# Hybrid attention laid out by row tile instead of by pair of heads, with the first tile's projection and expert choice between the second tile's jobs

## The chip, the cores and the metric

One core of a Trainium2 chip. The metric is the device time of the whole kernel in microseconds (us); lower is better.

## What is computed

A three-layer block on x of 256 tokens by 1024 features, all in float32. Layers 1 and 2 (differential attention, block attention, each with a squared-ReLU MLP) are untouched. Layer 3 is the hybrid layer:

```python
proj = rmsnorm(x, norm1_gain) @ w_in
o_a  = nsa_mixer(...)      # 8 heads: compressed, selected and window branches, gated
o_b  = mla_mixer(...)      # 8 heads over low-rank q and kv
mixed = concat([rmsnorm(o_a), rmsnorm(o_b)]) @ w_out
h = x + mixed
return h + peer_ffn(rmsnorm(h, norm2_gain), w_q, sub_keys, u, v)
```

`peer_ffn` does this for each of 256 tokens and 8 heads: a query (256 wide, RMS-normed), scores against two sets of 128 keys, the best 16 of each, the best 16 of the 256 sums, hence 16 experts out of 16384; then `sum_k softmax_k * gelu(x . u[e_k]) * v[e_k]`.

## The kernel before

Tokens are handled in two row tiles of 128. The engines have programs written out by hand, bound together by named semaphores; the order in each program is the order of work on that engine.

**Hybrid attention.** The eight selected and window head pairs and the four low-rank head pairs are 12 units (`nsa_unit`, `mla_unit`). A unit holds two heads m and three 128x128 blocks for each: tile 0 against keys 0, tile 1 against keys 0 and 1. TensorE's loop over u = 2..13 (L1137 on) turns the probabilities of unit u-2 (`turn_probs`, L632), makes the scores of unit u (`scores`, L623 and L625), and weighs the values of unit u-2 (`weigh`, L641 to L643), with one group of low-rank transposes (`turn_low_rank`, L1134) in eight of the steps. VectorE adds the mask and takes the row peak (`add_bias`, L1887), copies the turned probabilities of head 0 (L1901), inverts the totals (L2275, L2279) and scales the results into `nat` (`finish`, L2291, L2294). ScalarE takes the exponentials (L1279) and copies those of head 1 (L1285).

**Output projection and first choice** (`out_and_first_choice`, L916, and the start of `peer`, L958). The halves of the mixed rows are normed (ScalarE squares L1424, GpSimd power L1655, VectorE `out_scale` L2302), turned (L898) and multiplied by w_out: for each tile 16 matmuls of 128x512 (`out_product`, L906). Then for tile 0: add to `h` (L1993), turn (L863), query (L874), key scores (L889), and VectorE's choice (`first_choice`, L2458 to L2498), which names experts 0 to 7 (`first_names`, L2446) and then 8 to 15. Tile 1 goes through the same after its projection; its choice is laid between the dot products of tile 0's first unit (`unit`, L2520: key scores L2348, names L2423).

**The expert phase** (`peer`). There are 16 units (8 heads by 2 tiles), each of 16 gathers. One gather is an indirect DMA issued by GpSimd (L1772) of 128 rows of 8 KB, an expert's u and v side by side: 1.05 MB. There are 16 slots, one for each k. VectorE dots u with the row (L2506), ScalarE applies gelu (L1471) and makes a diagonal of the weights (L1459), TensorE adds v through it (`add_experts`, L838) and so frees slot k; the next unit's gather k waits for that (`v_used`) and for the names of its experts (`experts_ready`). SyncE also loads the 1.05 MB query weights of each further head (seven loads into ring slot 2, L379), the first when w_out is used up. The first unit's gathers are issued in `first_unit` on GpSimd (L1787), in an order that follows which slots are free:

```python
po.wait_ge(sem("experts_ready"), ...)    # experts 0..7 of tile 0
gather(0, 0..3); power(...); row_rms(1); gather(0, 4..7)
po.wait_ge(sem("experts_ready"), ...); po.wait_ge(sem("w_out_used"), ...)
gather(0, 8..10); po.wait_ge(sem("peer_q_done"), 4); gather(0, 11); power(...)
gather(0, 12..15)
```

## Time and profile before

| | us |
|---|---|
| Median of 3 runs | 1463.73 (1460.67 to 1466.08) |
| The profiled execution, its own time | 1461.87 |
| Its span, first to last instruction | 1460.1 |
| TensorE busy | 1323.1 (91%) |
| VectorE busy | 944.3 (65%) |
| ScalarE busy | 549.5 (38%) |
| GpSimd busy | 358.4 (25%) |

The profiled execution's time is its span plus 1.8 us around it. Busy shares are means over stages that differ: the MLPs and projections to about 700 us, the hybrid attention from 708 to 760 us, projection and first choice to about 828 us, the expert phase to the end.

### The profile page before, as it was taken

What the parts mean: (1) busy time and instruction counts of PE and PEld (TensorE: products, weight loads), DVE (VectorE), ACT (ScalarE), POOL (GpSimd) and SP (SyncE); (2) the same over time, 40 slices, a digit from 0 to 9 for tenths busy, and PEclk for the clock granted to TensorE, in tenths of its full rate; (3) what the DMA queues carried; (4) which work ended last, traced back from release to release, by engine and by line L of the source; (5) the groups of instructions that cost most, each with busy time, mean ns of one, the idle gap of its engine ahead of it and who ended that gap; (6) DMA issues with size and microseconds to landing.
All of it is one profiled execution on the core that took longest, in us unless ns stands there. A gap on an engine that the chain in (4) does not pass through costs nothing.

```text
span 1460.1 us, 19575 instructions
## 1 busy us (share of the span) xinstructions
PE 1323.1 (91%) x6461; PEld 934.2 (64%) x6461; DVE 944.3 (65%) x2283; ACT 549.5 (38%) x1131; POOL 358.4 (25%) x372
## 2 busy tenths in 40 slices
PE   8999999999999999999999789797887979788877
PEld 6988999988988999977875435343343535343333
DVE  4687554564557555585764777776767777776755
ACT  4563544444555444454662122222222212222221
POOL 0104000000000000012402454435434344345440
PEclk9999999999999999999999899899999999999999
DMA  9614665545315565463403999999999999999997
GB/s 360 261 58 113 226 196 172 195 151 231 116 55 174 176 191 183 167 235 123 174 1 124 420 420 421 420 421 422 422 421 422 422 422 422 421 422 422 421 421 306
DMA packets 97534, 406.84 MB, mean 279 GB/s; under 512 B 6955, under 2 KB 44524, under 8 KB 60748
## 3 DMA queue, kind: packets, MB, share of 16 engines
q0 software_dynamic: 39552, 276.60, 46.1%
q1 hardware_dynamic: 57932, 129.60, 25.9%
q8 instruction: 28, 0.46, 0.1%
q14 instruction: 22, 0.18, 0.0%
HBM read 404.84 MB, written 1.07 MB: 278 GB/s over the span
## 4 chain that ended last, share of the span: by engine, by line
PE 51%; DMA 22%; issue 13%; DVE 9%; POOL 2%; ACT 2%; DVEq 0%; POOLq 0%; SPq 0%; ACTq 0%
DMA arena_u<-in_peer_uv,prob 20%; PE ps L685 12%; PE ps L686 12%; PE ps L687 12%; PE ps L838 6%; DMA uv_gain<-in_peer_uv,prob 2%; PE ps L906 1%; DVE arena_u L2506 1%; PE ps L632 1%; PE ps L812 1%; PE ps L625 1%; PE ps L641 1%; DVE prob L2382 1%; DVE prob L2370 1%; PE ps L623 1%
## 5 line engine op out<-in xcount | busy, mean ns | idle before, releaser
L1860 DVE TENSOR_TENSOR w_low<-ring,w_high 128x1024 fp32r<-128x1024 f32 x140 | 165.2, 1221 | 151.3 <-ACT w_high L1222 150.8
L1222 ACT ACTIVATE w_high<-ring 128x1024 fp32r<-128x1024 f32 x140 | 140.7, 1052 | 171.8 <-PE ps L687 171.8
L838 PE MATMUL ps<-arena_u,sco 128*128 128x512 f32 x256 | 126.8, 648 | 36.1 <-ACT sco L1459 36.1
L685 PE MATMUL ps<-hT_high,w_high 128*128 128x256 f32 x512 | 145.0, 283 | 0.9 <-DVE hT_low L1853 0.9
L686 PE MATMUL ps<-hT_low,w_high 128*128 128x256 f32 x512 | 144.9, 283 | 0.0
L687 PE MATMUL ps<-hT_high,w_low 128*128 128x256 f32 x512 | 144.8, 283 | 0.0
L1471 ACT ACTIVATE prob<-prob 128x4 f32<-128x4 f32 (+2 forms) x67 | 13.8, 206 | 343.5 <-DVE prob L2506 343.5
L1459 ACT ACTIVATE sco<-const,prob 128x128 f32<-128x128 f32 x256 | 84.7, 392 | 155.1 <-DVE prob L2516 137.4
L1661 POOL TENSOR_SCALAR small<-small 128x1 f32<-128x1 f32 x8 | 4.3, 533 | 499.2 <-ACT arena_v L1254 499.2
L838 PEld LDWEIGHTS ps<-arena_u,sco 128*128 128x128 f32 x256 | 52.3, 208 | 102.7 <-issue 57.0
L838 PE MATMUL ps<-arena_v,sco 128*128 128x512 f32 x256 | 117.7, 592 | 0.0
L2506 DVE CUSTOM_DVE_ANT_0 arena_v<-arena_v,nat 128x1024 f32<-128x1024 f32 x64 | 78.4, 1226 | 57.4 <-DMA arena_v<-in_peer_uv,prob 56.8
L1772 POOL DMA_INDIRECT arena_u<-in_peer_uv,prob x64 | 75.8, 1185 | 157.7 <-DVEq L2425 67.2
L838 PE MATMUL ps<-ring,sco 128*128 128x512 f32 x192 | 89.9, 619 | 20.4 <-ACT sco L1459 20.4
L838 PE MATMUL ps<-uv_gain,sco 128*128 128x512 f32 x128 | 76.3, 752 | 34.4 <-ACT sco L1459 34.4
L2506 DVE CUSTOM_DVE_ANT_0 arena_u<-arena_u,nat 128x1024 f32<-128x1024 f32 x64 | 78.5, 1226 | 37.6 <-DMA arena_u<-in_peer_uv,prob 36.5
L685 PEld LDWEIGHTS ps<-hT_high,w_high 128*128 128x128 f32 x512 | 98.1, 192 | 2.4 <-DVE hT_low L1853 1.3
L686 PEld LDWEIGHTS ps<-hT_low,w_high 128*128 128x128 f32 x512 | 98.2, 192 | 1.0
L687 PEld LDWEIGHTS ps<-hT_high,w_low 128*128 128x128 f32 x512 | 98.2, 192 | 0.0
L685 PE MATMUL ps<-w_high,act_high 128*128 128x512 f32 x240 | 94.7, 394 | 0.0
L686 PE MATMUL ps<-w_low,act_high 128*128 128x512 f32 x240 | 94.3, 393 | 0.0
L687 PE MATMUL ps<-w_high,act_low 128*128 128x512 f32 x240 | 93.7, 391 | 0.0
(440 smaller groups left out, 2955.7 us busy)
## 6 DMA issues: line engine op xcount, KB each, us to landing
ring<-in_w_up SPq DMA_DIRECT2D x32, 1024.0 KB, 5.5
ring<-in_w_down SPq DMA_DIRECT2D x32, 1024.0 KB, 4.8
qkring<-in_qk_a SPq DMA_DIRECT2D x8, 1024.0 KB, 7.1
qkring<-in_qk_b SPq DMA_DIRECT2D x8, 1024.0 KB, 4.9
ring<-in_peer_wq SPq DMA_DIRECT2D x7, 1024.0 KB
ring<-in_w_in SPq DMA_DIRECT2D x8, 860.0 KB, 5.5
ring<-in_w_out_a SPq DMA_DIRECT2D x4, 1024.0 KB, 15.6
ring<-in_v_b SPq DMA_DIRECT2D x4, 1024.0 KB, 6.9
```

Source lines behind the costliest of these rows:

```text
L623: pe.matmul(ps[banks[m]][:, 0:P], q(m)[:, 0:P], k(m)[:, 0:P], start=True, stop=True)
L625: pe.matmul(ps[banks[m]][:, P:384], q(m)[:, P:S], k(m)[:, 0:S], start=True, stop=True)\
L632: last = pe.transpose(ps[2 + m][:, k * P:(k + 1) * P], prob[:, b, m, k * P:(k + 1) * P], ident)
L685: pe.matmul(dst, a[0], b[0], start=start, stop=False, skip_group_check=True)
L686: pe.matmul(dst, a[0], b[1], start=False, stop=False, skip_group_check=True)
L687: return pe.matmul(dst, a[1], b[0], start=False, stop=stop, skip_group_check=True)
L838: last = pe.matmul(ps[2 * t + n][:, :], diag[:, k % N_DIAG, :], slots[k][:, D + n * HALF:D + (n + 1) * HALF], start=False, stop=(final and ...
L1222: sc.activation(w_split[pair][0][:, part], ring[:, slot, part], ACT.Copy)\
L1459: sc.activation(diag[:, k % N_DIAG, :], ident, ACT.Copy, scale=weight[:, 16 * t + k:16 * t + k + 1])\
L1772: po.indirect_dma_start(slots[k], None, T["peer_uv"], bass.IndirectOffsetOnAxis(ap=expert[:, 16 * t + k:16 * t + k + 1], axis=0))\
L1860: ve.tensor_tensor(w_split[pair][1][:, part], ring[:, slot, part], w_split[pair][0][:, part].bitcast(F32), ALU.subtract)\
L2506: ve.tensor_tensor_reduce(row, row, nat[:, t, :], 1.0, 0.0, ALU.mult, ALU.add, dots[:, k:k + 1])\
```

## The change

The attention is cut into 18 jobs (`job_parts`). Jobs 0 to 5 hold tile 0 alone, two units in each (four blocks of 128x128); jobs 6 to 17 hold tile 1, one unit in each (two heads by 256 keys). All turned probabilities of a job go through one PSUM bank and one ScalarE copy of 512 columns; VectorE copies none. Scores of every job use the same two PSUM banks, so TensorE waits for the masking of the job before. Tile 0's norms, projection, row norm, query, key scores, choice and first gathers are laid into the steps of tile 1's jobs; tile 0 is turned and scored 128 columns at a time. Tile 1's last half, its rows, query and choice follow in `last_rows` and `first_unit`. The slots are renumbered so that the first gathers go where the attention holds nothing. The choice's scratch, the key scores' banks and ScalarE's outputs of the squares move to other buffers. The expert phase from the second unit on is the same. The core of the diff (ScalarE's loop over the jobs, which mirrors TensorE's, and the small helpers are left out):

```diff
-        slots = [au[:, 2048 * r:2048 * r + 2048] for r in range(4)]
-        slots += [uv_proj[:, :], av[:, 4096:6144], uv_mk[:, 0, :], uv_mk[:, 1, :], ring[:, 0, :], ring[:, 1, :], ring[:, 3, :],
-                  first_wq, uv_gain[:, 0, :], uv_gain[:, 1, :], av[:, 6144:8192], av[:, 0:2048]]
+        slots = [au[:, 0:2048], au[:, 6144:8192], av[:, 4096:6144], av[:, 6144:8192], au[:, 2048:4096], au[:, 4096:6144],
+                 uv_proj[:, :], uv_mk[:, 0, :], uv_mk[:, 1, :], uv_gain[:, 0, :], av[:, 0:2048], ring[:, 0, :], ring[:, 1, :],
+                 ring[:, 3, :], first_wq, uv_gain[:, 1, :]]
...
+        def job_parts(j):
+            if j < FIRST_JOBS:
+                return [(x, 2 * j + x // 2, x % 2, x * P, (x + 1) * P) for x in (0, 2, 1, 3)]
+            return [(m, j - FIRST_JOBS, m, m * S, (m + 1) * S) for m in range(2)]
...
+            def last_rows():
+                pe.wait_ge(sem("finished"), count.take("finished"))
+                for n, bank in enumerate((2, 3)):
+                    turn_keys(range(2 + 4 * n, 6 + 4 * n), bank)
+                turn_out(1, 1, 6)
+                turn_keys(range(10, 14), 1)
+                turn_keys(range(14, 2 * P_HEADS), 0)
                 pe.wait_ge(sem("out_turned"), count.take("out_turned"))
+                for n in range(2):
+                    out_products(1, n, 4 + n, 1)
                 pe.wait_ge(sem("acc_ready"), count.take("acc_ready", 4))
                 pe.sem_inc(sem("w_out_used"), 1)
                 pe.sem_inc(sem(f"ring{PEER_SLOT}_used"), 1)
+                turn_rows(1, (7, 6))
+                first_queries(1, (4, 5), lambda c: hT[:, c, P:S])
+                pe.wait_ge(sem("pq_ready"), count.take("pq_ready", 4))
+                first_squares(1, 7)
+                first_scores(1, 6)
...
+                def job_scores(j):
+                    t = 0 if j < FIRST_JOBS else 1
+                    if j:
+                        pe.wait_ge(sem("sco_ready"), count.take("sco_ready", len(job_parts(j - 1))))
+                    parts = sorted(job_parts(j))
+                    for x, u, m, a, z in parts:
+                        q, k, _ = units[u]
+                        last = pe.matmul(score_places(j)[x], q(m)[:, t * P:(t + 1) * P], k(m)[:, 0:z - a], start=True, stop=True)
+                        if x >= len(parts) - 2:
+                            last.then_inc(sem("scores_ready"), 1)
...
+                def weigh_job(j):
+                    pe.wait_ge(sem("probT_a"), count.take("probT_a"))
+                    if j >= 2:
+                        pe.wait_ge(sem("finished"), count.take("finished"))
...
+                for step in range(2, N_JOBS + 2):
+                    j = step - 2
+                    if step == 9:
+                        turn_out(1, 0, 3)
+                    turn_job(j)
+                    if step in (4, 5):
+                        wait_low_rank(2)
+                    if step == MLA_JOB:
+                        wait_low_rank()
+                    if step == MLA_JOB + 2:
+                        wait_low_rank()
+                    if step < N_JOBS:
+                        job_scores(step)
+                    if step == 8:
+                        pe.wait_ge(sem("keysT_ready"), count.take("keysT_ready"))
+                        turn_out(0, 0, 3)
+                    if step == 12:
+                        pe.wait_ge(sem("pq_ready"), count.take("pq_ready", 4))
+                        first_scores(0, 0)
+                    if step == 18:
                         pe.wait_ge(sem("out_turned"), count.take("out_turned"))
+                        out_products(1, 0, 4, 0)
+                    if step == 19:
+                        out_products(1, 1, 5, 0)
+                    weigh_job(j)
+                    if step == 3:
+                        pe.wait_ge(sem("mqk_ready"), count.take("mqk_ready", 2))
+                        turn_low_rank(0, 0, 0)
+                        turn_low_rank(1, 0, 1)
+                    if step == 4:
+                        turn_low_rank(2, 0, 3)
+                        turn_low_rank(3, 0, 0)
+                    if step == 5:
+                        turn_keys((0, 1), 3)
+                    if step == 8:
+                        for n in range(2):
+                        pe.wait_ge(sem("out_turned"), count.take("out_turned"))
+                        for n in range(2):
+                            out_products(0, n, n, 0)
+                    if step == 9:
+                        pe.wait_ge(sem("out_turned"), count.take("out_turned"))
+                        for n in range(2):
+                            out_products(0, n, n, 1)
+                    if step == 10:
+                        turn_rows(0, (3, 0))
+                    if step == 11:
+                        first_queries(0, (1, 3), lambda c: hT_first[:, c, :])
+                    if step == 12:
+                        first_squares(0, 3)
+                        turn_low_rank(0, 1, 1)
+                    if step == 13:
+                        wait_low_rank()
+                        turn_low_rank(1, 1, 1)
+                    if step == 14:
+                        turn_low_rank(2, 1, 1)
+                    if step == 15:
+                        wait_low_rank()
+                        turn_low_rank(3, 1, 1)
+                    if step == 17:
+                        pe.wait_ge(sem("key_scores_taken"), count.take("key_scores_taken"))
+                        turn_out(0, 1, 3)
+                last_rows()
...
+            def last_rows():
+                half_squares(1, 1)
...
+                gates_of(0, scale=ms_out[:, 0:1])
+                row_squares(1)
+                take_rows(1, 6)
+                first_queries(1, (4, 5))
+                gelu_of(0, 4)
+                diagonals(0, range(4), first=True)
...
+                po.wait_ge(sem("c_out"), count.take("c_out", 2))
                 po.wait_ge(sem("experts_ready"), count.take("experts_ready"))
                 alone()
                 for k in range(4):
                     gather(0, k)
                 power(ms_out[:, 0:1], ms_in[:, 0:1], "ms_ready", "rms_ready")
+                po.wait_ge(sem("m_turned_a"), count.take("m_turned_a", 8))
+                for k in range(4, 6):
+                    gather(0, k)
+                half_rms(1)
+                count.skip("weighed", 2 * N_LAYER_UNITS)
+                po.wait_ge(sem("weighed"), count.take("weighed", N_JOBS))
+                gather(0, 6)
+                half_rms(3)
+                gather(0, 7)
+                po.wait_ge(sem("experts_ready"), count.take("experts_ready"))
+                gather(0, 8)
+                po.wait_ge(sem("keysT_ready"), count.take("keysT_ready", 6))
+                alone()
+                for k in range(9, 11):
+                    gather(0, k)
+                po.wait_ge(sem("w_out_used"), count.take("w_out_used"))
+                for k in range(11, 14):
+                    gather(0, k)
                 row_rms(1)
                 po.wait_ge(sem("peer_q_done"), count.take("peer_q_done", 4))
                 alone()
+                gather(0, 14)
                 power(ms_out[:, 1:2], ms_in[:, 1:2], "ms_ready", "rms_ready")
                 po.wait_ge(sem("rows_scaled"), count.take("rows_scaled"))
+                gather(0, 15)
...
+                for step in range(2, N_JOBS + 2):
+                    j = step - 2
+                    if step == 10:
+                        add_out(0, 0)
+                    job_share(j)
+                    if step < N_JOBS:
+                        job_bias(step)
+                    if step == 7:
+                        out_scale(0, 0)
+                    if step == 8:
+                        out_scale(1, 0)
+                    if step == 12:
+                        first_choice_begun()
+                    if step == 17:
+                        out_scale(0, 1)
+                    finish_job(j)
+                    if step in (5, 7, 15):
+                        ve.sem_inc(sem("norm_due"), 1)
+                    if step == 10:
+                        take_rows(0, 3)
+                    if step == 13:
+                        then(row_scale(0))
+                        first_query_rms(0)
+                        first_choice_ended()
+                    if step == 15:
+                        ve.wait_ge(sem("rms_ready"), count.take("rms_ready"))
+                        ve.tensor_scalar(neg_top, top[:, 0:1], ms_out[:, 0:1], -1.0, ALU.mult, ALU.mult)\
+                            .then_inc(sem("top_ready"), 1)
+                ve.sem_inc(sem("norm_due"), 1)
+                dot(0, 0)
+                dot(0, 1)
+                out_scale(1, 1)
+                dot(0, 2)
+                dot(0, 3)
+                dot(0, 4)
+                add_out(1, 4)
+                take_rows(1, 7)
+                gates_in(0)
+                dot(0, 5)
+                row_scale(1).then_inc(sem("rows_scaled"), 1)
+                dot(0, 6)
+                weights_of(0, 0, 4)
+                first_query_rms(1)
...
+            def first_unit():
+                dot(0, 7)
+                first_key_scores(1)
+                first_eights(1)
+                second_eights()
+                best_pairs()
+                dot(0, 8)
+                weights_of(0, 4, 8)
+                next_pairs()
+                pick(0)
+                pick(1)
+                name_experts(1)
+                for k in range(9, 13):
+                    dot(0, k)
```

## Rows read from the trace of the kernel before

**Rows 1.** The page, 40 equal slices: what the DMA engines moved.

```profile
GB/s 360 261 58 113 226 196 172 195 151 231 116 55 174 176 191 183 167 235 123 174 1 124 420 420 421 420 421 422 422 421 422 422 422 422 421 422 422 421 421 306
```

**Rows 2.** Stretches: PE, PEld, DVE, ACT, POOL busy, PEclk, DMA share, GB/s.

```profile
720.00:740.00 20.00, 19.98 (x174) 17.30 (x173) 16.97 (x89) 15.52 (x59) 0.00 (x0) 1.00 0.01 2
900.00:1000.00 100.00, 85.74 (x225) 41.62 (x224) 66.09 (x184) 22.80 (x66) 45.91 (x41) 0.93 1.01 421
```

**Rows 3.** Stretches of 2 us, gathers' begin and end, same columns.

```profile
790.00:792.00 2.00, 2.00 (x8) 1.04 (x8) 1.64 (x14) 0.00 (x0) 1.70 (x2) 1.00 0.46 66
792.00:794.00 2.00, 1.84 (x5) 0.53 (x3) 1.78 (x11) 0.00 (x0) 1.39 (x3) 1.00 0.76 279
...
1448.00:1450.00 2.00, 0.73 (x3) 0.27 (x2) 0.99 (x4) 0.90 (x3) 0.00 (x0) 1.00 0.38 156
```

**Rows 4.** Timeline of POOL: first gather of the first two units.

```profile
789.75 1.10 POOL L1772 DMA_INDIRECT arena_u<-in_peer_uv,prob  x1 [9.00 <-DVEq L2448]
...
828.02 1.26 POOL L1772 DMA_INDIRECT arena_u<-in_peer_uv,prob  x1 [11.19 <-DVEq L2425]
```

**Rows 5.** The chain of waits: start, us, what it ran on.

```profile
723.62 0.66 PE ps L632 x6
724.27 0.42 PE ps L623 x4
724.69 0.43 PE ps L625 x4
...
725.49 0.22 PE ps L642 x2
...
726.61 0.44 PE ps L1134 x4
...
742.12 0.87 PE ps L625 x4
...
767.67 6.87 PE ps L906 x16
...
779.07 3.57 PE ps L874 x32
```

**Rows 6.** Timeline of DVE: tile 0's choice, first and second part.

```profile
784.95 0.49 DVE L2458 MAX8 prob<-ps 128x8 f32<-128x128 f32 x2
...
788.61 0.17 DVE L2446 SCALAR_TENSOR_TENSOR prob<-prob 128x8 uint32<-128x8 f32 x1
788.96 0.06 DVE L2326 MEMSET small<- 128x1 f32 x1 [0.18 <-DVE prob L2446]
...
795.19 0.17 DVE L2446 SCALAR_TENSOR_TENSOR prob<-prob 128x8 uint32<-128x8 f32 x1
```

**Rows 7.** Groups by line, 700 to 835 us: busy us, mean ns.

```profile
L1417 ACT ACTIVATE hT<-ps 128x512 f32<-128x512 f32 x4 | 2.4, 591 | 5.1 <-PE ps L898 5.1
...
L2506 DVE CUSTOM_DVE_ANT_0 arena_u<-arena_u,nat 128x1024 f32<-128x1024 f32 x4 | 4.9, 1226 | 0.1
```

**Rows 8.** Timeline of PE and DVE, attention's start to tile 1's names.

```profile
716.73 0.87 PE L632 MATMUL ps<-const,prob 128*128 128x128 f32 x6 [0.79 <-DVE nat L2266]
...
760.10 1.10 DVE L2294 TENSOR_SCALAR nat<-ps,share 128x64 f32<-128x64 f32 x4 [2.66 <-PE ps L643]
...
763.14 0.66 PE L898 MATMUL ps<-const,nat 128*128 128x128 f32 x4 [1.38 <-DVE nat L2302]
...
790.16 3.68 PE L906 MATMUL ps<-ring,hT 128*128 128x512 f32 x8
...
811.20 0.48 DVE L2348 TENSOR_SCALAR sco<-ps,small 128x256 f32<-128x256 f32 x1 [3.96 <-POOL small L1655]
...
826.89 0.17 DVE L2423 SCALAR_TENSOR_TENSOR prob<-prob 128x16 uint32<-128x16 f32 x1
```

**Rows 9.** Stretches of 1 us: PE busy us, PEclk, DMA share, GB/s.

```profile
815.00:816.00 1.00, 0.00 (x0) 0.50 1.02 426
...
824.00:825.00 1.00, 1.00 (x2) 0.57 1.01 418
```

391 lines of the change are left out of this document (178 added, 213 removed).

## The prediction

> **What bounds the kernel now.** I read the page first. Its row of DMA rates stands at 420 to 422 GB/s in every slice from the 23rd to the 39th and was far lower before [rows 1]: from about 800 us to the end the gathers fill the DMA engines, while in the same stretch TensorE is busy 85.7 of 100 us and VectorE 66 [rows 2]. So the expert phase is a stream with a fixed amount left to carry, and the end moves only with the time at which the stream runs and with the gaps in it. One gather, or one load of query weights, is 1.05 MB, at 421.5 GB/s 2.49 us. There are 256 gathers and 7 loads: 263 pieces, 654 us. In the stretches of 2 us where it starts the engines move 66 and 279 GB/s, in the two together 2.4 us less than at full rate, so the full rate counts from 792.4 us; in 1448 to 1450 they move 156 GB/s, so it ends near 1448.7 [rows 3]. That is 656.3 us, the 654 and two for small gaps and the store. The first gather was issued at 789.75 [rows 4]: from issue to full flow the start costs 2.65 us.
>
> Ahead of that, from 716.7 to 794 us, TensorE sets the pace: in 720 to 740 us it is busy 19.98 of 20 us, VectorE 16.97 [rows 2], and the chain of waits there runs almost wholly on it [rows 5]. Nothing moves on the DMA engines in that stretch (2 GB/s).
>
> **What the change can win.** There are 16 slots, so no more than tile 0's 16 gathers can go ahead of tile 1's names. In the kernel before, the 17th gather is issued at 828.0 [rows 4], before the first 16 have been carried (792.4 + 39.8 = 832.2): no gap. In the changed kernel the 16 are spread over the attention's second half and its tail, and the first load of query weights (freed when w_out is used up) goes with them: 17 pieces are out of the way when tile 1's names come. If they come late there is a pause, and then 246 pieces remain. With T as the issue of tile 1's first gather, full flow counts from T + 2.65, against 792.4 + 17 x 2.49 = 834.7 before. So the end moves by T - 832.05, earlier or later, and the whole question is T. The early gathers cost nothing of themselves: the engines that carry them were empty [rows 2].
>
> The Trainium skill (DMA: Bandwidth & Descriptors, Anatomy of one DMA) gives about 2.0 us of fixed cost for one DMA. By it the restart would be 0.65 us cheaper than by the row, and the end 0.65 us earlier than I sum it; the row decides.
>
> **T, part by part.** A float32 matmul leaves two records, a transpose one.
>
> (a) *TensorE's work between the attention's first turn and its last weighing.* The first turn was at 716.7 [rows 8]; masking job 0 is 0.3 us less on VectorE ahead of it, so 716.4. The total of turns, scores and weighings is the same (72 transposes, 72 small matmuls, the same columns). 72 turns at 0.11 (six took 0.66): 7.9. 72 weighings at 0.22 to 0.23: 16.2. A unit's scores took 0.85 for 768 columns; a job has 512, but keeps the start, 0.75, for ten jobs, and the six low-rank ones 0.87 (two of 256 columns): 12.7. Eight low-rank groups at 0.44: 3.5 [rows 5]. What is now laid between: 24 matmuls with w_out (tile 0's 16, half of tile 1's) at 0.86 (eight took 6.87), 20.6; tile 0's query 3.6 [rows 5]; three turns of mixed rows at 0.44, row turns, key turns, key scores and squares, all by the same prices, 3.1. Sum 67.6 us.
>
> (b) *Waits inside.* ScalarE now copies 512 columns for every job, 0.59 [rows 7], with hand-over about 0.85, over 0.75 of scores; in tile 0's jobs it also has four exponentials and two low-rank copies, 3.1 us against TensorE's 2.9; the masking must be done before the next scores, because the banks are not doubled. Between nothing (all covered by the work laid between) and 1 us each I take 0.4, 16 times: 6.5. VectorE's choice is the large one. It is in line between masks: the first part took 3.8 us (784.95 to 788.8) and lies in step 12; the second 6.4 (788.96 to 795.4) [rows 6], with the row scale and the query's square in front 7.8, in step 13. TensorE there has a weighing, a low-rank group and a turn, 1.5 us each time, and then needs the next mask: 2.3 and 6.2 us idle, and 0.8 more as the loop closes up. Sum 15.8 us. In the kernel before the same choice cost TensorE nothing: it was covered by the w_out matmuls, which are spent now. Last weighing done: 716.4 + 67.6 + 15.8 = 799.8, where it was 760.0.
>
> (c) *From there to tile 1's names.* Before, the turn of the mixed rows started 3.0 us after the last weighing [rows 8]; now two dots of 1.23 [rows 7] are queued on VectorE ahead of the scale, 3.7: 803.5. Turn and copy 1.3, eight w_out matmuls 6.9: 811.7. Before, 17.4 us passed from the end of these matmuls (790.16 + 3.7) to VectorE's key scores (811.20) [rows 8], since tile 0's choice and nine gathers were in VectorE's and GpSimd's queues. Now: add, three gathers on GpSimd, row norm 5.3; row scale 1.3; dot, square, norm behind gather 14, and a last dot 3.7: 10.3, so 822.0. The choice took 15.8 (811.20 to 827.06) with five dots in it [rows 8]; now one is left: 10.9. Names at 832.9, first gather 0.95 later as before (827.06 to 828.02): 833.9.
>
> (d) *The clock.* TensorE's granted clock fell to 0.50 (1.2 GHz) in 815 to 816, after it had stood idle from 812, and was back at 2.4 GHz only in 825, 3.6 us after it had resumed [rows 9]. The 6 us stall in step 13 can do this. Half speed for 3.6 us loses at most 1.8, and nothing if it does not fall: 1.2. The Trainium skill (Perfetto Trace Analysis, Matmul Optimizations) wants matmuls back to back in batches because power follows utilization; that speaks against this interleaving and would take the 1.8.
>
> (e) The same bookkeeping laid over the kernel before gives its names 0.9 us too early; with more hand-overs now I add 1.5.
>
> T = 833.9 + 1.2 + 1.5 = 836.6, and the end moves by 836.6 - 832.05 = +4.6 us. After the restart I expect no further gap: TensorE frees a slot in 1.72 us (two matmuls of 0.86), the stream takes 2.49. The pause itself: the 16th gather is carried by about 830, full flow returns at 839. The profiled execution's 1461.87 becomes 1466.5; the median stood 1.9 us above it, so 1463.73 + 4.6 = **1468.3 us**, +0.3%. I call within 0.5% (7.3 us) no change.
>
> **Rivals.**
> 1. *The job loop is paced by hand-overs* (slower). Each job passes TensorE, VectorE, ScalarE and back with one set of banks, and VectorE was already busy 17 of 20 us with 12 units [rows 2]. At 0.8 us of wait per step in place of 0.4, T is 6.4 later: +11.0, 1474.7. It decides from +2.7 us of waits, 0.17 per step. Against it: VectorE loses its copies of the turned probabilities.
> 2. *TensorE stays full* (faster). If jobs turned and scored ahead cover the choice and ScalarE's copies, 12.7 of the 15.8 us go: T = 823.9, -8.1 us, 1455.6; all of it gone, -11.2, 1452.5. For it: the total work is unchanged and the loop before had waits of only 0.2 us. Against it: the scores of the next job need VectorE's mask, and VectorE is in the choice.
> 3. *The order changes nothing at the end*: names come at the time that 832 asks, and the gap just closes. This is inside my forecast's own band.
>
> **How the numbers follow.** Forecast (waits within about 3 us of mine) 0.56, rival 1 0.27, rival 2 0.17. The range takes (b) at 0.1 to 1 us per step (-5, +9), the clock at 0 to 1.8 and the calibration at 0 to 3: 1457 to 1477. Rival 2's far end is left out, and what lies beyond 1477. Faster by over 0.5% 0.17, within 0.56, slower 0.27.
>
> **What the profile after would show.** Right: gathers 0 to 3 issued near 770, DMA rate back to zero for 7 to 10 us before full flow near 839; TensorE idle for 5 us and more in front of one job's scores, released by VectorE's mask, with the DVE in the choice's lines; a last weighing at 798 to 803; from its end to tile 1's names 33 to 35 us. Wrong: the stream full before 835, or TensorE idle under 10 us in the attention (rival 2); the idle spread evenly over all steps (rival 1); or a second gap after the restart, which would mean that slots come free too slowly, a cost that none of my cases holds.

## The result, and the profile after

The changed kernel takes **1479.32 us** (median of 4 runs, 1476.31 to 1480.78) against 1462.28 (1460.67 to 1466.08, 4 runs) for the kernel before on the same chip: ratio 1.011, 95% interval 1.0082 to 1.0138. It is slower by 17.0 us, where 4.6 were forecast. The profiled execution took 1478.41 us, its span is 1476.6, against 1461.87 and 1460.1.

First the page's rates over 40 slices, which answer to [rows 1]: the stream is the same, it only fills two slices later (313 and 385 GB/s in the 23rd and 24th).

```profile
PEclk9999999999999999999898999999999989898999
...
GB/s 359 256 57 106 227 196 172 198 143 228 114 65 165 180 190 190 151 241 108 172 1 171 313 385 420 421 421 421 422 422 421 422 421 421 421 422 421 421 421 316
```

The stretches around the restart (columns as in [rows 2]). The DMA engines are empty at 848 to 850, carry 291 GB/s in 852 to 854 and the full rate behind that; in the steady state (the last row) nothing has changed.

```profile
790.00:792.00 2.00, 1.20 (x3) 1.02 (x4) 1.46 (x8) 1.56 (x6) 0.00 (x0) 0.50 1.02 430
846.00:848.00 2.00, 2.00 (x10) 1.58 (x9) 1.83 (x8) 0.95 (x3) 0.00 (x0) 1.00 0.06 25
848.00:850.00 2.00, 2.00 (x11) 1.77 (x10) 1.71 (x5) 0.00 (x0) 0.00 (x0) 1.00 0.00 0
850.00:852.00 2.00, 2.00 (x6) 0.81 (x5) 2.00 (x5) 0.89 (x3) 1.28 (x2) 1.00 0.41 61
852.00:854.00 2.00, 2.00 (x6) 0.95 (x5) 2.00 (x5) 0.67 (x3) 1.96 (x1) 1.00 0.70 291
900.00:1000.00 100.00, 86.72 (x231) 43.08 (x230) 73.78 (x227) 21.80 (x61) 45.02 (x40) 0.97 1.01 421
```

POOL's timeline, tile 0's first gather and tile 1's, answering to [rows 4]. The first came 9.6 us earlier than before, the second, which is T, 22.4 us later.

```profile
780.14 1.10 POOL L1880 DMA_INDIRECT arena_u<-in_peer_uv,prob  x1 [1.67 <-issue]
...
850.41 1.26 POOL L1880 DMA_INDIRECT arena_u<-in_peer_uv,prob  x1 [11.27 <-DVEq L2584]
```

TensorE's timeline (start, us, then what it ran; in brackets the idle time before it and what ended it) shows where T became late: the head, the choice, and the last stretch. L552 are the idle transposes that the kernel has there anyway.

```profile
710.56 2.00 PE L1101 MATMUL ps<-arena_u,hT 128*128 128x60 f32 x16
712.48 0.72 PE L1116 MATMUL ps<-hT 64*128 64x128 f32 x8
715.66 0.72 PE L1116 MATMUL ps<-hT 64*128 64x128 f32 x8 [2.46 <-DVE peak L2346]
716.31 2.81 PE L552 MATMUL ps<-const 128*128 128x128 f32 x12
...
723.40 0.66 PE L1125 MATMUL ps<-const,prob 128*128 128x128 f32 x4 [0.79 <-DVE nat L2393]
...
728.95 1.97 PE L1135 MATMUL ps<-proj,probT 128*128 128x64 f32 x8
...
782.46 1.13 PE L1116 MATMUL ps<-qkring 96*128 96x256 f32 x4 [2.23 <-ACT qkring L1656]
...
790.80 2.08 PE L1116 MATMUL ps<-qkring 96*128 96x256 f32 x4 [5.50 <-DVE peak L2346]
792.67 1.84 PE L1135 MATMUL ps<-proj,probT 128*128 128x64 f32 x8
...
811.28 1.00 PE L1135 MATMUL ps<-val,probT 128*128 128x64 f32 x8
...
816.60 1.11 PE L918 MATMUL ps<-const,nat 128*128 128x128 f32 x4 [3.44 <-DVE nat L2432]
...
818.78 8.72 PE L927 MATMUL ps<-ring,hT 128*128 128x512 f32 x16
```

The same eight weighing records take 1.97 us at 728.95, 1.84 at 792.67 and 1.00 at 811.28. The stretches of TensorE alone (busy us, granted clock, DMA share, GB/s) say why: in four places the granted clock goes to 0.50, that is 1.2 instead of 2.4 GHz, each time behind waits.

```profile
716.00:720.00 4.00, 4.00 (x27) 0.57 0.95 335
...
728.00:730.00 2.00, 2.00 (x13) 0.50 0.00 0
...
792.00:796.00 4.00, 4.00 (x19) 0.50 0.19 80
...
816.00:818.00 2.00, 1.40 (x7) 0.50 0.70 295
```

In step s TensorE turns and weighs job s-2 and makes the scores of job s, so the weighings run from step 2 to step 19. Two marks carry the rest of this text. **C** is the start of the compressed branch's scores on TensorE (L1101, 710.56 above), the beginning of what the change touches. **T** is the issue of tile 1's first gather. In the kernel before C is 706.65 and T 828.02: 121.4 us. After the change: 139.85.

### The profile page after: what moved, and what is told of

It reads as the page before. It is cut to its first block, busy times and chain, and to the rows that moved or that the text cites. A ratio compares the mean times of both kernels' runs of the same rounds, so it can differ in the third digit from the quotient of the medians.

```text
span 1476.6 us, 19592 instructions
## 1 busy us (share of the span) xinstructions
PE 1343.0 (91%) x6461; PEld 948.0 (64%) x6461; DVE 939.8 (64%) x2271; ACT 555.4 (38%) x1137; POOL 365.8 (25%) x372
## 4 chain that ended last, share of the span: by engine, by line
PE 56%; DMA 22%; DVE 10%; issue 8%; ACT 2%; POOL 1%; DVEq 0%; SPq 0%; POOLq 0%; ACTq 0%
DMA arena_u<-in_peer_uv,prob 20%; PE ps L706 13%; PE ps L707 13%; PE ps L708 13%; PE ps L859 5%; PE ps L927 2%; DMA ring<-in_peer_uv,prob 2%; PE ps L1135 1%; PE ps L1116 1%; PE ps L653 1%; PE ps L552 1%; DVE arena_u L2670 1%; DVE prob L2541 1%; DVE qkT L2529 1%; PE ps L662 1%
## 5 line engine op out<-in xcount | busy, mean ns | idle before, releaser
L859 PE MATMUL ps<-arena_u,sco 128*128 128x512 f32 x256 | 137.0, 685 | 39.2 <-ACT sco L1535 39.2
L1547 ACT ACTIVATE prob<-prob 128x4 f32<-128x4 f32 (+2 forms) x67 | 13.8, 206 | 324.0 <-DVE prob L2670 319.4
L859 PE MATMUL ps<-ring,sco 128*128 128x512 f32 x192 | 95.2, 637 | 28.4 <-ACT sco L1535 28.4
L1880 POOL DMA_INDIRECT arena_u<-in_peer_uv,prob x64 | 72.7, 1136 | 167.1 <-DVEq L2584 72.2
L2670 DVE CUSTOM_DVE_ANT_0 arena_v<-arena_v,nat 128x1024 f32<-128x1024 f32 x64 | 78.5, 1228 | 37.1 <-DMA arena_v<-in_peer_uv,prob 36.2
L2670 DVE CUSTOM_DVE_ANT_0 arena_u<-arena_u,nat 128x1024 f32<-128x1024 f32 x64 | 78.4, 1226 | 37.1 <-DMA arena_u<-in_peer_uv,prob 35.8
L2670 DVE CUSTOM_DVE_ANT_0 ring<-ring,nat 128x1024 f32<-128x1024 f32 x48 | 58.6, 1224 | 63.1 <-DMA ring<-in_peer_uv,prob 63.1
```

What stands on the lines that cost most here:

```text
L859: last = pe.matmul(ps[2 * t + n][:, :], diag[:, k % N_DIAG, :], slots[k][:, D + n * HALF:D + (n + 1) * HALF], start=False, stop=(final and ...
L1880: po.indirect_dma_start(slots[k], None, T["peer_uv"], bass.IndirectOffsetOnAxis(ap=expert[:, 16 * t + k:16 * t + k + 1], axis=0))\
L2670: ve.tensor_tensor_reduce(row, row, nat[:, t, :], 1.0, 0.0, ALU.mult, ALU.add, dots[:, k:k + 1])\
```

## The experiments

Every kernel but the two with delays and the two controls is the changed kernel with the edit named; the diffs are shortened to what matters. The table gives the profiles' own marks, one execution for each kernel. Columns: C; from C to the start of the weighing of step 2; from there to that of step 5; steps 14 to 17, the sum of the four intervals between weighings; from the end of the last weighing to T; C to T; span less T; and the timed median of the kernel, beside that of the kernel before in the same set.

| kernel | C | C to step 2 | 2 to 5 | 14 to 17 | last to T | C to T | span - T | median, before |
|---|---|---|---|---|---|---|---|---|
| changed | 710.56 | 15.20 | 12.66 | 22.13 | 38.13 | 139.85 | 626.2 | 1479.3, 1462.3 |
| e10_after_again | 710.63 | 15.00 | 14.02 | 21.39 | 37.09 | 139.24 | 626.2 | 1478.2, 1464.0 |
| e1_choice_cover | 710.88 | 15.03 | 13.98 | 16.76 | 38.09 | 135.60 | 626.1 | 1470.1, 1465.6 |
| e2_warm | 707.81 | 15.28 | 10.53 | 26.28 | 35.71 | 139.53 | 626.5 | 1476.1, 1465.6 |
| e3_head | 710.80 | 12.24 | 15.05 | 23.83 | 37.12 | 140.14 | 626.1 | 1475.6, 1465.6 |
| e4_first_late | 707.73 | 15.16 | 12.71 | 22.10 | 37.25 | 143.34 | 626.2 | 1483.6, 1465.6 |
| e7_head_warm | 711.18 | 12.24 | 10.63 | 23.81 | 37.10 | 136.84 | 626.2 | 1473.0, 1465.9 |
| e9_choice_clock | 713.26 | 15.02 | 14.00 | 21.13 | 37.28 | 139.10 | 626.0 | 1474.2, 1464.0 |
| e14_pool_order | 710.87 | 15.18 | 12.66 | 22.11 | 38.14 | 139.88 | 626.1 | 1478.6 (one run) |
| e15_late_dot | 708.48 | 15.21 | 12.65 | 22.12 | 36.84 | 138.57 | 626.9 | 1475.7 (one run) |
| e16_choice_clock_2 | 706.09 | 15.16 | 12.83 | 20.07 | 38.71 | 138.44 | 626.3 | 1472.6 (one run) |
| e11_all_no_warm | 713.05 | 15.00 | 14.02 | 14.06 | 36.06 | 130.88 | 627.7 | 1471.0, 1464.0 |
| e8_all | 706.18 | 12.24 | 10.63 | 12.90 | 36.03 | 123.54 | 627.4 | 1459.7, 1465.9 |
| e12_all_queries | 713.33 | 12.23 | 10.64 | 14.04 | 34.41 | 123.06 | 626.9 | 1463.2, 1464.0 |
| e5_before_4 | 709.47 | | | | | 126.74 | 628.0 | 1466.6, 1465.9 |
| e6_before_14 | 710.87 | | | | | 139.27 | 627.9 | 1478.6, 1465.9 |
| e13_before_again | 706.26 | | | | | 121.36 | 632.1 | 1463.2, 1463.7 |

### Does T alone set the end?

**e5_before_4, e6_before_14**: nothing of the change, only its supposed effect.

```diff
+                if first:
+                    for _ in range(14):      # 4 in e5_before_4
+                        then(ve.tensor_reduce(settled, h[:, 0, :], X, ALU.min))
                 name_experts(1 - t)
```

> The kernel before, with 4 idle reductions over 128x1024 values on VectorE ahead of the naming of tile 1's first experts, about 1.3 us each (from the 1.22 us of the dots of the same size). Nothing else is changed. Theory (the end is the issue of tile 1's first gather, T, plus a fixed 626.2 us, once T is later than about 833.9; up to there the transfers of tile 0's gathers cover it): T goes from 828.0 to about 833.2 and the time does not move, 0 to +1 over the kernel before. Rival (VectorE's chain is on the path one to one in the kernel before too): +5.2.

> The same with 14 of the reductions, about 18 us. Theory: T at about 846, span 846 + 626.2 = 1472, time +12 over the kernel before; so the kernel before with nothing but this delay takes about as long as the changed kernel. Rival 1 (one to one): +18. Rival 2 (the changed kernel's loss comes from something else than T, and the stream has slack for a late start): under +3.

Measured: e5_before_4 1466.59, +0.7 us by the medians, ratio 1.0015 (1.0004 to 1.0027), so at most +4.0 us, where its one to one rival asked +5.2; its profile has T at 836.21 and not at 833.2, because that execution's C was 2.8 us late. e6_before_14 1478.63, +12.8, ratio 1.0086 (1.0058 to 1.0113), with 14 reductions in 17.5 us. VectorE's timeline of e6_before_14, and then POOL's with T:

```profile
831.45 17.52 DVE L2512 TENSOR_REDUCE small<-h 128x1 f32<-128x1024 f32 x14
```

```profile
850.14 1.26 POOL L1772 DMA_INDIRECT arena_u<-in_peer_uv,prob  x1 [28.75 <-DVEq L2425]
```

The one to one rival (+18) falls, and so does slack for a late start (under +3). The kernel before with this delay has its T at 850.14, where the changed kernel has 850.41, and takes as long: 1478.6 and 1479.3. A late T alone thus costs as much as the whole change. Span less T is 627.9 and 628.0 with a delay; by that the span of 1460.1 belongs to T = 832.1 to 832.2, the forecast's 832.05. In the changed kernels span less T is 626.0 to 627.7, for T from 829.7 to 852.4. Where the 1.7 us between 627.9 and 626.2 lie, TensorE's stretches behind T show, first of e6_before_14 and then of the changed kernel: against 421.5 GB/s the first is short by 3.2 us of full flow in these 10 us, the second by 1.8.

```profile
850.14:854.14 4.00, 1.75 (x2) 0.50 0.50 152
854.14:860.14 6.00, 6.00 (x26) 0.89 0.98 377
```

```profile
850.41:854.41 4.00, 4.00 (x11) 1.00 0.68 229
854.41:860.41 6.00, 6.00 (x27) 1.00 1.00 421
```

**e4_first_late**: gathers 0 to 3 issued together with 4 and 5.

```diff
-                for k in range(4):
-                    gather(0, k)
                 power(ms_out[:, 0:1], ms_in[:, 0:1], "ms_ready", "rms_ready")
                 po.wait_ge(sem("m_turned_a"), count.take("m_turned_a", 8))
-                for k in range(4, 6):
+                for k in range(6):
                     gather(0, k)
```

> The changed kernel with tile 0's first four gathers issued together with its fifth and sixth, at about 794 instead of 780. Theory (only T counts, as long as all 16 gathers of tile 0 are in before the names of tile 1 are ready: 16 pieces of 2.49 us are 40 us, from 794 on they would be in by about 840, before T at 850): no change, 1479.3 within 1. Rival 1 (each gather that starts earlier is worth its transfer): 4 of 2.49, slower by 10, 1489. Rival 2 (they disturb less this way, since gathers and the weights' loads no longer share the queues at 780): faster by 1 to 2.

Measured: 1483.62, ratio 1.0125 (1.0107 to 1.0144), 4.3 us over the changed kernel by the medians. The theory's number missed, yet not by the rival's mechanism: span less T is 626.2 as ever, and T itself is 3.5 us later after C. Six issues on POOL now stand ahead of its normalisation (L1858), which starts 92.5 us after C; in the changed kernel, behind two, it started at 799.93, 89.4 after C. TensorE waits 3.35 us for the scale behind it, in step 18 (interval 10.58, for 6.18). POOL's timeline of e4_first_late, and then TensorE's:

```profile
799.21 0.93 POOL L1880 DMA_INDIRECT arena_u<-in_peer_uv,prob  x1 [0.30 <-issue]
800.21 0.19 POOL L1858 TENSOR_SCALAR small<-small 128x1 f32<-128x1 f32 x1
```

```profile
801.99 0.96 PE L918 MATMUL ps<-const,nat 128*128 128x128 f32 x4 [3.35 <-DVE nat L2430]
```

An early gather is worth nothing to the stream here; a moved one costs by the queue it stands in.

### The choice

**e1_choice_cover**: the long part of the choice under the out products.

```diff
                     if step == 13:
-                        then(row_scale(0))
+                        ve.wait_ge(sem("rms_ready"), count.take("rms_ready"))
                         first_query_rms(0)
-                        first_choice_ended()
+                        first_choice_ended()      # to the replacements only
+                    if step == 18:
+                        first_choice_rest()
+                    if step == 19:
+                        then(scale_row(0))
```

> The changed kernel with one part moved: of tile 0's choice the first three replacements stay in step 13, the rest of it (from the second maxima to the names 8 to 15, some 5 us on VectorE) goes to step 18 and the row scaling (1.28 us) to step 19, where VectorE waits 5.56 and 4.11 us for the out products. Theory (the two-part choice stops the jobs and drops the clock, both land on T, the issue of tile 1's first gather, and the end moves one to one with T): the 5.5 us idle before the scores at 790.80 shrinks to under 1 us and the 8.1 us of work between 790.8 and 798.9 that ran at half the clock takes about 4.3 us less, so T goes from 850.4 to about 841, time 1470 (1468 to 1472.5). Rival 1 (the choice's stall only, the clock falls elsewhere instead): T 845, time 1474. Rival 2 (the end hangs on something else than T, such as the row gathers' own order): 1479, unchanged.

Measured: 1470.12 (10 runs), ratio 1.004 (1.0022 to 1.0057), the time that the theory gave. The profile does not show the theory's T of 841: that execution took 1474.4 and has T at 846.48, which is rival 1 (845, 1474). The stop is gone and steps 14 to 17 went from 22.13 to 16.76 us, but the clock fell all the same, behind the 2.23 us wait of step 14 (0.50 in 784 to 790), and longer in the early jobs.

**e9_choice_clock, e16_choice_clock_2**: the choice stays, the stop is filled with idle transposes: 40 in step 15, in the second kernel also 16 in step 14.

```diff
+                    if step == 14:                       # e16_choice_clock_2 alone; weigh_job(12) no longer waits for it
+                        pe.wait_ge(sem("finished"), count.take("finished"))
+                        keep_turning(6, 16)
+                    if step == 15:
+                        pe.wait_ge(sem("key_scores_taken"), count.take("key_scores_taken"))
+                        keep_turning(0, 40)
...
                     if step == 17:
-                        pe.wait_ge(sem("key_scores_taken"), count.take("key_scores_taken"))
```

> The changed kernel with the choice where it is and 40 idle transposes (about 5.1 us) on TensorE in step 15, in the 5.5 us in which it waits for VectorE's choice; the wait for the choice's scores to be taken moves from step 17 to step 15, where it has long been met. Theory (this stop costs twice: the 5.5 us, and about 4.3 us because the work from 790.8 to 798.9 runs at half the clock after it): the wait stays, the clock stays at 1.00, the time 4.3 less, 1475 (1473.5 to 1476.5). Rival 1 (what ran at half the clock was covered by ScalarE and VectorE): unchanged, 1479. Rival 2 (the fall only moves to a later place): 1477.

> e9_choice_clock with 16 more idle transposes in step 14, in the 2.2 us before the low-rank copies are ready; in e9_choice_clock the clock fell in that wait already and the 40 of step 15 ran at half of it. Theory (the clock's part of the choice is a cost of its own): the clock at 1.00 from 778 to 800, the four intervals of steps 14 to 17 together 22.1 (changed kernel) less 3.2 = 18.9, and T as much earlier. Rival (the chain through VectorE and ScalarE covers it): 21 to 22.

Measured: e9_choice_clock 1474.17 (1469.89 to 1480.2), ratio 1.0069 (1.0043 to 1.0096), against 1.011 (1.0087 to 1.0132) for the control of the same set; these two intervals overlap. Its profile is of the slowest of these executions and shows no gain (steps 14 to 17: 21.13, the control 21.39): the clock had gone to 0.50 in the wait before, in step 14, and the 40 transposes ran at half speed. With that wait filled too, e16_choice_clock_2 keeps 1.00 throughout:

```profile
776.00:780.00 4.00, 3.51 (x28) 1.00 0.59 174
780.00:784.00 4.00, 4.00 (x39) 1.00 1.00 414
784.00:788.00 4.00, 2.47 (x17) 1.00 1.02 430
788.00:792.00 4.00, 3.55 (x26) 1.00 0.27 64
792.00:796.00 4.00, 3.59 (x27) 1.00 0.87 326
```

and the four intervals come to 20.07 us. That is 2.1 less than 22.13 and 1.3 less than the control's 21.39, where the theory said 3.2 and the rival 0.1 to 1.1. So by one execution of each the fall behind the choice costs 1.3 to 2.1 us, besides the stop; that part of the slow work was covered by waits is a reading and not shown by itself.

### The head, the early jobs, the last stretch

**e3_head, e2_warm, e7_head_warm.**

```diff
                 job_scores(0)
+                keep_turning(7, 18)       # e3_head, e7_head_warm
                 job_scores(1)
-                keep_turning(7, 12)
...
+                keep_turning(0, 5)        # e7_head_warm: before the wait for the compressed outputs
...
+                    if step == 2:         # e2_warm: before the turn
+                        keep_turning(0, 6)
...
+                    if step == 5:         # e2_warm, e7_head_warm: before the scores
+                        keep_turning(1, 5)
...
+                    if step in (2, 3):    # e2_warm, e7_head_warm: before the weighing
+                        keep_turning(0, 5)
...
+                        keep_turning(2, {14: 10, 15: 34}[step])    # e2_warm: before the scores, behind a wait for probT_a
...
+                keep_turning(0, 24)       # e2_warm: before tile 1's last turn
                 turn_out(1, 1, 6)
```

> The changed kernel with the second job's scores behind the warm-up transposes at the head (18 of them between the two jobs' scores, in place of 12 after both), so that TensorE has work while VectorE takes the first job's scores. Theory (the single pair of score banks stops TensorE 2.46 us there, its clock falls to 0.50 and the first turn of the jobs is about 2.8 us late; this is on the path to T): first turn about 2.8 us earlier, time 1476.5 (1475.5 to 1477.5). Rival 1 (the head is bounded by the compressed branch's probabilities, not by this): 1479, unchanged. Rival 2 (a first fall of the clock avoided also avoids the second one at 726.8): 1473.

> The changed kernel with idle transposes of the identity on TensorE inside waits it has anyway: 6 and 5 in step 2, 5 in step 3, 5 in step 5, 10 in step 14, 34 in step 15, 24 before tile 1's last turn of the outputs. Nothing else is moved. Theory (falls of the granted clock to 0.50 are a cost of their own, beside the waits): the stretches 726.8 to 733.8, 790.8 to 798.9 and 815.8 to 822 come back to full clock and give 3.5, 4 and 2.5 us, less 1 to 3 us where the inserted turns overrun their wait: T earlier by 7, time 1472 (1469.5 to 1475). Rival 1 (the slower TensorE is covered by waits for the other engines, so that only their chain counts): 1478 to 1480. Rival 2 (the inserted turns lengthen the chain more than the clock gives): over 1481.

> The changed kernel with the head's order of e3_head and idle transposes in the early jobs: 5 before the wait for the compressed branch's outputs, 5 in steps 2, 3 and 5, all of them in waits of 0.5 to 0.8 us. Theory (the head's gain of 2.9 us was lost again in e3_head because the clock stayed at 0.50 for 13 us after it instead of 7; with the clock held both gains stand): first turn about 12.8 less 2.9 after the compressed scores' start, step 6 at 30 or less after it less 3, T 5.5 to 6 us earlier than in the changed kernel, time 1473.5 (1472 to 1475). Rival (the gain is eaten by a later fall, or the early jobs are bound by the other engines): 1476 to 1479.

Measured: e3_head 1475.6, ratio 1.0066 (1.0048 to 1.0084); e2_warm 1476.09, 1.0073 (1.0055 to 1.0091); e7_head_warm 1472.95, 1.0045 (1.0023 to 1.0067). The head's order is worth 3.0 us to step 2 (15.20 to 12.24), but in the profile of e3_head the clock then stays at 0.50 through 736 and takes 2.4 us back before step 5, and steps 14 to 17 take another 1.7. That execution, the slowest of its four, thus shows C to T no shorter (140.14), though the median time is 3.7 us under the changed kernel's. With a few transposes in the waits it stays up, and steps 2 to 5 take 10.63 instead of 12.66 us, transposes included. In e2_warm those placed at the choice made it worse (26.28): they had to wait for ScalarE's copy, which stands behind the next job's exponentials, so they ran after the stop and not in it. The 24 ahead of the last turn shortened the last stretch by 2.4 us against the first profile of the changed kernel (35.71 for 38.13), by 1.4 against the second (37.09); without any it is 37.1 to 38.7 from one execution to the next. In e7_head_warm the gain of 5.0 to step 5 is followed by 3.0 us of loss from step 14 to 18 (23.81 for 22.13, and a step 18 of 7.52 for 6.18). TensorE's rows of 778 to 802 us, of e7_head_warm and then of the changed kernel, show that this is the clock, at half for the whole stretch:

```profile
778.00:802.00 24.00, 20.65 (x77) 0.51 0.66 258
```

```profile
778.00:802.00 24.00, 15.79 (x87) 0.79 0.64 243
```

It fell behind the 2.23 us wait of step 14. The changed kernel has the same wait and kept 1.00 there; what decides between the two is not settled.

**e14_pool_order, e15_late_dot**: half_rms(3) ahead of gather(0, 6); dot(0, 8) and the weights behind name_experts(1).

> The changed kernel with one thing moved: POOL normalises tile 1's low-rank half first and issues gather 6 of tile 0 after it, not before. Theory (the issue of one gather, 1.2 us on POOL, stands ahead of the scale that tile 1's last turn waits for, and this chain is on the path to T): from the last weighing's end to T 38.1 less 1.2, from the compressed scores to T 139.5 less 1.2 = 138.3. Rival 1 (two dots on VectorE hold the turn for as long anyway): 139.5. Rival 2 (without the wait the clock doesn't fall there either): 136.5.

> The changed kernel with the dot of expert 8 and the weights 4 to 8 behind the names of tile 1 instead of inside them. Theory (from the key scores to the names VectorE is alone on the path; the dot is 1.22 us and the weights 0.2): from the key scores on TensorE to T 14.9 less 1.4 = 13.5, from the compressed scores to T 138.1. Rival (the names wait for something else, TensorE or POOL): 14.9, unchanged.

Measured, in one run each: the first changes nothing (last weighing to T 38.14). In the changed kernel the gather's issue ended at 813.58 and ScalarE's squares, for which POOL's normalisation waits, at 813.60, so POOL lost nothing by it. The second takes 1.3 us out of the last stretch (36.84; 1.4 were expected); but span less T grows from 626.2 to 626.9, so half of it is given back.

### Together, and the controls

**e8_all** has the edits of e7_head_warm, the choice in four parts, the 24 transposes, and the edits of the last two kernels; **e11_all_no_warm** only the schedule: the choice in four parts and the last two edits, with the head's old order and no added transposes; **e12_all_queries** adds keep_turning(2, 12) ahead of tile 1's queries.

```diff
+                    if step == 13:
+                        first_choice_named()
                     finish_job(j)
...
+                    if step == 14:
+                        first_choice_ended()
```

> Everything together on the changed kernel: the head and early jobs of e7_head_warm; tile 0's choice in four parts (values in step 12, first names in step 13, replacements in step 14, the rest in step 18, the row scaling in step 19); 24 idle transposes before tile 1's last turn; POOL's gather 6 behind the normalisation instead of ahead of it; the dot of expert 8 behind the names. Theory (T alone moves the end, slope one, until it is earlier than the transfers of tile 0's 16 gathers): 850.4 less 6 (head and early clock), 9 (choice and its clock), 2.4 (tail clock), 1.2 (POOL), 1.6 (dot): T about 830, span 1456, time 1458 (1455 to 1463), faster than the kernel before by 0.3%. Rival 1 (the gains overlap, since fewer waits shift the clock's falls): T 836, time 1464. Rival 2 (T under 834 is of no use here either, the transfers of the gathers hold the end): 1462.

> e8_all without the idle transposes and with the head's old order: only the choice in four parts, POOL's gather 6 behind the normalisation, the dot of expert 8 behind the names. It tells how much of e8_all's 20 us is schedule and how much the clock. Theory: 7.7 us of stops at the choice and the 4.3 us of half-clock work behind them go, 2.6 us from POOL and the dot, the rest (head 2.9, early clock 3, tail clock 2.4) stays lost: T 836, time 1465 (1463 to 1467). Rival (without the idle transposes a fall comes at the choice anyway, as in e1_choice_cover): T 840, time 1469.

> e8_all with 12 more idle transposes in the 1.74 us before tile 1's queries, which took 5.44 us there for the 3.8 us that they take at full clock. Theory (T binds in e8_all, slope one): T 828.1, time 1.6 less, 1458.1. Rival (at T under 830 the transfers of tile 0's gathers bind): same as e8_all, 1459.7.

Measured: e8_all 1459.7 (10 runs), ratio to the kernel before 0.997 (0.9953 to 0.9986); e11_all_no_warm 1471.02, 1.0048 (1.0031 to 1.0065); e12_all_queries 1463.15, 0.9986 (0.9969 to 1.0002). TensorE in e8_all meets the choice with waits of 0.31 and 0.61 us where the changed kernel had 5.50:

```profile
774.26 1.13 PE L1117 MATMUL ps<-qkring 96*128 96x256 f32 x4 [0.31 <-DVE peak L2352]
776.00 1.10 PE L1136 MATMUL ps<-proj,probT 128*128 128x64 f32 x8 [0.61 <-ACT probT L1675]
...
799.34 7.13 PE L927 MATMUL ps<-ring,hT 128*128 128x512 f32 x16
```

C to T falls by 16.3 us: head 3.0, early jobs 2.0, choice 9.2, last stretch 2.1. The 20.2 expected counted the POOL order's 1.2, which is nothing, and the clock fell once more, at tile 1's queries (5.44 us where 3.8 are needed). e11_all_no_warm stands 7.3 us behind in the same measure, its theory's time (1465) 6 us too low, the rival's (1469) near: of the 16.3 some 9 us are schedule and 7 the head's order and the clock. e12_all_queries takes 1.6 us out of the last stretch and yet C to T is only 0.5 shorter, steps 14 to 17 having taken 1.1 more; its time, 1463.2, is neither the theory's 1458.1 nor the rival's 1459.7. The repaired order is thus at best 0.3% faster than the kernel before, and by e12_all_queries perhaps not at all.

**e10_after_again, e13_before_again.** Both kernels unchanged.

> The changed kernel itself once more, as a control beside the others and for a second profile. Theory (the 3 to 4 us by which everything ahead of the hybrid attention was late in its first profile are falls of the clock at 100 to 125 and 425 to 450 us that come and go from execution to execution, in code that the change doesn't touch): time 1479.3 within 2; the start of the compressed scores at 707 to 711, and from it to T the same 139.9 us as in the first profile, within 1. Rival (that lateness is a result of the change): the start at 710.6 again in every execution and never in the kernel before.

> The kernel before itself once more, for a second profile. Theory (the start of the compressed scores moves between 706 and 713 from execution to execution in every kernel of this study, with falls of the clock ahead of it, in code that the change leaves alone; the first profile of the kernel before was one of the early ones): time 1460 to 1468 like the kernel before, the start later than 706.65 by 1 to 5 us, the stretch from it to T still 121.4 within 0.5. Rival (the kernel before has no falls up there, so that the 3.9 us are the change's): the start at 706.7 again.

Measured: 1478.21 (ratio 1.011, 1.0087 to 1.0132) and 1463.19 (0.9998, 0.9981 to 1.0015). C to T repeats to 0.6 us after the change and to 0.01 before it. The parts of it repeat less well: the changed kernel's two profiles differ by 1.4 us in steps 2 to 5, 0.7 in steps 14 to 17 and 1.0 in the last stretch, so a price read from one part of one profile is no better than that. C was again early in the kernel before (706.26, which was not expected) and again late in the changed one (710.63). But that isn't bound to the change: the kernel before with a delay has 709.47 and 710.87, and e16_choice_clock_2 and e8_all, with the changed order, 706.09 and 706.18. C goes with falls of the clock further up. The four profiles without any (before, e13_before_again, e16_choice_clock_2, e8_all) have it at 706.1 to 706.7; in others the clock falls in 100 to 125 us, in 400 to 450 us (e10_after_again: 0.94 and 0.93) or in both. The rows of 100 to 125 us, first of the changed kernel and then of e16_choice_clock_2:

```profile
100.00:125.00 25.00, 22.61 (x121) 0.86 0.29 48
```

```profile
100.00:125.00 25.00, 22.42 (x132) 1.00 0.27 53
```

## Why the prediction was wrong

**The mechanism held.** The full stream, the restart behind a pause, T as the one lever, and the break-even of 832.05 were right; the delayed kernels before show 832.1 to 832.2. With the measured T the formula gives 850.41 - 832.05 = +18.4, the profiled pair has +16.5. Some 0.8 of those 1.9 us is the restart: it was put at 2.65 us, and by the rows of the 10 us behind T it cost 1.8 us of full flow in the changed kernel. The other 1.1 is not accounted for. In e6_before_14 the restart cost 3.2 us, so that the formula meets the delayed kernels to 0.2 us is in part luck: a restart 0.5 us dearer than it holds stands against something cheaper. The Trainium skill (DMA: Bandwidth & Descriptors, Anatomy of one DMA) gives about 2.0 us of fixed cost for one DMA. The 1.8 lies near it, but that is no confirmation: by the same section most of the 2.0 passes behind the last byte, and the stretch here lies ahead of full flow.

**What failed is T**, 836.6 in the forecast and 850.4 on the chip, 13.8 us:

| | forecast | measured | more |
|---|---|---|---|
| first turn | 716.4 | 723.40 | 7.0 |
| first turn to end of last weighing (a, b) | 83.4 | 88.9 | 5.5 |
| from there to T (c) | 34.1 | 38.1 | 4.0 |
| clock, calibration (d, e) | 2.7 | in the rows above | -2.7 |

Of the signs that the forecast named, the gap in the stream is there (some 7 us of it), and the stop of over 5 us released by VectorE's mask; but the first gathers came at 780 and not near 770, and the last weighing ended at 812.3, not by 803.

- *The clock (d), the largest.* I asked only whether the one long stop makes it fall, and took 1.2 us, at most 1.8. It fell four times. Against the first profile the runs give: the head 1.3 (twelve idle transposes in 2.81 us, where eighteen take 2.18 in e3_head, 0.12 each), the early jobs 2.0 (e7_head_warm), the choice 2.1 (e16_choice_clock_2), the last stretch 2.4 (e2_warm), together 7.8 us. Against the second profile the last three are 3.4, 1.3 and 1.4, together 7.4 with the head's 1.3. The sum is firmer than its parts. The Trainium skill (Perfetto Trace Analysis, Matmul Optimizations) advises matmuls back to back in batches. The trace agrees, the price being these 7 to 8 us.
- *The work (a) was put too low, the waits (b) too high.* TensorE's rows from the first turn to the end of the last weighing, of the changed kernel and then of e8_all, where the clock stays at 1.00:

```profile
723.40:812.28 88.88, 77.09 (x440) 0.90 0.19 72
```

```profile
716.05:793.69 77.64, 72.60 (x455) 1.00 0.21 82
```

  Less its fifteen idle transposes (1.9 us) e8_all does the same work in 70.7 us, where (a) has 67.6; the weighings take 17.5 us of it and not 16.2. The changed kernel was idle for 11.8 us there, where (b) has 15.8, and its slow clock stretched the 70.7 to 77.1. So the 5.5 us are 3.1 of work, 6.4 of clock and 4.0 less of waits: the clock's net price in this stretch, the 4.1 above, is less than 6.4 because slow work fills waits. That last reading is argued and not shown.
- *The head was left out.* "The banks are not doubled" stands in (b), but I did not apply it ahead of the first turn, where the second job's scores now wait 2.46 us for the first job's mask. That is most of the 3.1 us beyond C, its share of the clock included.
- *C, 3.9 us*, lies in code that the change leaves alone and moved between 706.1 and 713.3 in these profiles. Like for like, C to the end takes 753.4 us before and 766.0 after: 12.6 us are the attention's. Timed, the two sets gave 17.0 and 14.3. Whether what is over 12.6 is more than scatter stays open.
- *The choice in (b) was sized well.* Forecast 2.3, 6.2 and 0.8 us idle, 9.3 in all; measured 2.23 and 5.50, with 1.3 to 2.1 us of clock on top. Laid elsewhere it gives 9.2 back in e8_all and 8.1 in e11_all_no_warm and e12_all_queries. That it costs nothing under the w_out matmuls was right too: e1_choice_cover put it there, and its step 18 (6.18) and last stretch (38.09) are as long as before.
- *(c)*: of the 4.0 us, 1.4 to 2.4 are the clock. All but 0.3 of them lie ahead of VectorE's key scores (at 838.22); from there to T it took 12.2 us, where 11.9 were forecast. The dots ahead of the scale were not the cost I feared: the scale waited for POOL's normalisation until 815.79, after both.

Of the rivals none came true as described. Rival 1 gave the nearest time, 1474.7, but by waits in every step; here TensorE waited 0.57, 0.65 and 0.33 us in the whole of steps 6 to 13, and the loss sat at the head, in steps 2 to 5, at the choice and in the last stretch.

The range was also narrower than its own terms. Its upper ends (+9, +0.6 and +1.5 over 1468.3) add up to 1479.4, where it stops at 1477. The measured 1479.3 is what these ends give together, but the sizes are not theirs: they put it on waits in every step.

## What to carry to other kernels

Moving work earlier pays only if it moves the event that releases the bottleneck. Find that event (here one gather), and confirm it by a plain delay in the old kernel before judging a new order. When a covered piece of vector work is laid between short matmul jobs, count three things: the wait, the slow clock behind it, and the same again wherever banks are single. Put such work under the longest run of matmuls, in pieces no longer than the gap. Compare executions from a mark where the changed code begins.

## What was not expected of the hardware

- Waits far shorter than the 5.5 us stop were followed by half clock too: behind 2.46 us at 713 to 716, and behind 0.79, 0.18 and 0.81 us close together at 722 to 726. In e3_head, with the second set alone, 0.50 lasted through 736. In e7_head_warm, with the head's order in place of the first wait and five idle transposes, about 0.7 us, in those of the second set, it was 1.00 from 706 to 742.
- The same wait need not have the same result. Behind the 2.23 us of step 14 (released by ScalarE's copy) the clock went to 0.50 in e1_choice_cover, e7_head_warm, e9_choice_clock and e10_after_again, and stayed at 1.00 in the changed kernel's first profile, e3_head, e14_pool_order and e15_late_dot.
- The same unchanged code reaches C after 706.1 to 713.3 us, from one execution to the next, with the clock in 100 to 125 us at 1.00, 0.93 or 0.86 and in 425 to 450 us at 0.87 to 1.00.
- Span less T goes with how many of tile 0's dots are left behind tile 1's names: 626.0 to 626.5 us with seven, 626.9 to 627.7 with eight, 627.9 to 628.0 with nine. Between seven and nine, 1.4 of the 1.7 us lie in the 10 us behind T. Why is not shown.
